# Decay sums of a gated linear attention by a VectorE scan in place of a triangular matmul, with two products re-ordered

## The chip, the cores and the metric

One Trainium2 chip, eight cores. The batch has eight sequences and every core computes one of them alone, with the whole set of weights; the cores exchange nothing. The metric is the device time in microseconds of the slowest core. Engines are named TensorE (PE), VectorE (DVE), ScalarE (ACT), GpSimd (POOL) and SyncE (SP). Each works off its own list of instructions.

## The reference

A layer of a decoder: a half-step SwiGLU, a mixer, cross-attention into 256 memory tokens, a second half-step SwiGLU, a final norm. Widths: model 1024, sequence 4096, hidden 2816. The change touches the mixer's gated linear attention alone. It has four heads with keys of 128 and values of 256, and computes, per head,

```
log_a = logsigmoid(a_code @ w_alpha + b_alpha) / 16          # per token and key channel
b     = cumsum(log_a) within a chunk                         # cumulative log decay
o     = (q*exp(b)) @ (k*exp(-b))^T (causal) @ v  +  (q*exp(b)) @ state
state = exp(b_last) * (state + (k*exp(-b))^T @ v)
o     = rmsnorm over the 256 values of a head, times silu(r)
```

The second line is what the change computes in another way. The kernel works in chunks of 128 tokens where the reference has 64; the value is the same.

## The kernel before, in words

**Tiling.** Activations lie transposed, channels on partitions and tokens along the free dimension. The sequence is cut into four tiles of T = 1024 tokens. Each tile goes through first SwiGLU, mixer, cross-attention and second SwiGLU. Weights stream from HBM into five slots of 1 MB (in bf16), by DMAs issued from GpSimd's queue.

**Order of the work.** There is no planner: `Sched` writes for every engine one list of instructions in the order in which the Python code calls `S.op` and `S.mm`, and puts a semaphore wait before an instruction where a buffer that it reads or writes was last touched by another engine. So the order of the calls is the order on each engine, and whoever stands behind a waiting instruction on its engine waits too.

**PSUM.** `psum()` (line 306) hands out the eight banks in turn. In the recurrence `first_bank[0] = 2`: banks 0 and 1 are kept for the chunk's output (`B_o`), and all other products share six banks in turn. A product must therefore wait until the product six places before it in the order of calls has been read out.

**The recurrence** (label mix/gla, the loop `for i in range(12)`) works on the eight chunks of a tile as a software pipeline. In step i it calls, in this order: `B_norm(i-4)` (sum of squares over a head on PE with `onesV`, Ln and Exp on ACT into `rsn`, and then two DVE products that scale the output from banks 0 and 1 into `ogT`); `A1(i)` (the forget-gate projection, one 512-column matmul, then Exp into `zb` and Ln into `lp` on ACT, which gives the negative log of the decay); a fill; `A2(i-1)` (four 128-column matmuls with the triangle `triB`, which sum `lp` over the tokens of the chunk; Exp into `eb` and into `enb` on ACT; on DVE q times `eb`, k times `enb`; on GpSimd a copy of the last column into `ebl`); a fill; `A3(i-2)` (four score matmuls and four transposes of k on PE, masking on DVE, copy into `kg` on ACT); `B_kv(i-3)` (four 256-column matmuls into two banks, four DVE updates of the state, a GpSimd product `Sbf`); in steps 3 to 8 another fill; `B_o(i-3)` (sixteen 128-column matmuls into banks 0 and 1, square on ACT into `osq`); from step 3 on another fill; in steps 0 to 3 `pool(3-i, 1)`, the trailing sums of the other branch, two to five DVE instructions.

**Fills** are whole projection groups for PE, eight 512-column matmuls and one read-out each, taken from a list: values of chunks 0 and 1, then q and k of the tile's second half in turn, values of chunks 2 to 7, then the output gate r. Read-outs of values and of r alternate between ACT and DVE (`evac`, line 582); those of q are on ACT, those of k on DVE. In steps 1 to 8 the first fill of a step is read out by ACT, the second by DVE, the third by ACT and the fourth by DVE.

Of the kernel before, what the change touches and what calls it, by code (L numbers as in the profile page):

```python
# [7 lines left out]
F32 = mybir.dt.float32  # L8
BF16 = mybir.dt.bfloat16
AF = mybir.ActivationFunctionType  # L10
ALU = mybir.AluOpType
# [156 lines left out]
def build_program(nt=SEQ // T):  # L168
    nc = bass.Bass("TRN2", target_bir_lowering=False)
    S = Sched(nc)  # L170
# [28 lines left out]
    def sb(name, shape, dt):  # L199
        return nc.alloc_sbuf_tensor("sb_" + name, list(shape), dt)  # L200
# [26 lines left out]
    wa = sb("wa", [128, 256], BF16)  # L227
    identB = sb("identB", [128, 128], BF16)
    triB = sb("triB", [128, 128], BF16)
    onesD = sb("onesD", [128, 128], BF16)  # L230
    onesV = sb("onesV", [128, 128], BF16)
    walpha = sb("walpha", [128, 512], BF16)
# [8 lines left out]
    def ov(name, off_k, shape, dt, nb=1):  # L241
        esz = 4 if dt == F32 else 2
        size = int(np.prod(shape[1:])) * esz
        lo = int(off_k * 1024)
        hi = lo + size
        assert hi <= ARENA, (name, hi)
        t = nc.alloc_sbuf_tensor_at("ov_" + name, list(shape), dt, offset=abase + lo)
        bufs = [Buf(f"{name}{i}") for i in range(nb)]
        for (l2, h2, b2) in overlay:
            if l2 < hi and lo < h2:  # L250
                for b in bufs:
                    for o in b2:
                        b.alias.append(o)
                        o.alias.append(b)
        overlay.append((lo, hi, bufs))
        return t, bufs
# [18 lines left out]
    ogT, og_b = ov("ogT", 49, [128, 8, T], BF16, nb=8)  # L275
    dfT, df_b = ov("dfT", 65, [128, 4, T], BF16, nb=8)
    aT, aT_b = ov("aT", 73, [128, T], BF16, nb=2)
    lp2 = [ov(f"lp{i}", 75 + i, [128, 512], BF16) for i in range(2)]
    zb2 = [ov(f"zb{i}", 77 + 2 * i, [128, 512], F32) for i in range(2)]
    eb2 = [ov(f"eb{i}", 81 + 2 * i, [128, 4, 128], F32) for i in range(2)]  # L280
    enb2 = [ov(f"enb{i}", 85 + 2 * i, [128, 4, 128], F32) for i in range(2)]
# [24 lines left out]
    def psum():  # L306
        lo = first_bank[0]
        i = lo + bank_rr[0] % (8 - lo)
        bank_rr[0] += 1
        return banks[i], bank_b[i]  # L310
# [27 lines left out]
    def xload(i, src, reads=()):  # L338
        st, b = xs[i]
        S.dma("pool", [(st[:], src)], reads, b, f"dma:xs{i}")  # L340
        return st, b[0]
# [14 lines left out]
    wa_b = Buf("walpha")  # L356
    cb2 = Buf("const2")
    S.op("dve", lambda e: e.memset(onesD[:], 1.0 / 1024.0), [], [cb2])
    S.op("dve", lambda e: e.memset(onesV[:], 1.0 / 256.0), [], [cb2])
    S.op("dve", lambda e: e.tensor_copy(out=identB[:], in_=small[:, O_IDENT:O_IDENT + 128]), [const_b], [cb2])  # L360
    S.op("dve", lambda e: e.tensor_copy(out=triB[:], in_=small[:, O_TRI:O_TRI + 128]), [const_b], [cb2])
    CB = [const_b, cb2]
# [306 lines left out]
    def mixer(t, n1):  # L669
# [11 lines left out]
        v4 = lambda ap: ap.rearrange("p (a b) -> p a b", a=4)  # L681
# [87 lines left out]

        def A1(c):  # L770
            zb, zb_b = zb2[c % 2]
            lp, lp_b = lp2[c % 2]
            bz, bzb = psum()
            S.mm([(bz[:], aT[:, c * 128:(c + 1) * 128], walpha[:], True, True)], [aT_b[c // 4], wa_b], [bzb])
            S.op("act", lambda e: e.activation(out=zb[:], in_=bz[:], func=AF.Exp, scale=-1.0), [bzb], zb_b)  # L775
            S.op("act", lambda e: e.activation(out=lp[:], in_=zb[:], func=AF.Ln, bias=1.0), zb_b, lp_b)

        def A2(c):
            lp, lp_b = lp2[c % 2]
            eb, eb_b = eb2[c % 2]  # L780
            enb, enb_b = enb2[c % 2]
            tk = slice(c * 128, (c + 1) * 128)
            bc, bcb = psum()
            S.mm([(bc[:, h * 128:(h + 1) * 128], lp[:, h * 128:(h + 1) * 128], triB[:], True, True) for h in range(4)],
                 lp_b + CB, [bcb])
            S.op("act", lambda e: e.activation(out=eb[:], in_=v4(bc[:]), func=AF.Exp, scale=-1.0 / 16.0), [bcb], eb_b)
            S.op("act", lambda e: e.activation(out=enb[:], in_=v4(bc[:]), func=AF.Exp, scale=1.0 / 16.0), [bcb], enb_b)
            S.op("dve", lambda e: e.tensor_tensor(out=qT[:, :, tk], in0=qT[:, :, tk], in1=eb[:], op=ALU.mult),
                 eb_b, [qT_b[c]])
            S.op("dve", lambda e: e.tensor_tensor(out=kTt[:, :, tk], in0=kTt[:, :, tk], in1=enb[:], op=ALU.mult),  # L790
                 enb_b, [kT_b[c]])
            S.op("pool", lambda e: e.tensor_copy(out=ebl[:, c, :], in_=eb[:, :, 127]), eb_b, [ebl_b[c]])

        def A3(c):
            tk = slice(c * 128, (c + 1) * 128)
            sm, sm_b = sm3[c % 3]
            kg, kg_b = kg3[c % 3]
            bs, bsb = psum()
            S.mm([(bs[:, h * 128:(h + 1) * 128], kTt[:, h, tk], qT[:, h, tk], True, True) for h in range(4)],
                 [kT_b[c], qT_b[c]], [bsb])  # L800
            bt, btb = psum()
            btv = bt[:].bitcast(BF16)
            S.tr([(btv[:, h * 128:(h + 1) * 128], kTt[:, h, tk], identB[:]) for h in range(4)], [kT_b[c]] + CB, [btb])
            S.op("dve", lambda e: e.tensor_tensor(
                out=v4(sm[:]), in0=v4(bs[:]), in1=triB[:].unsqueeze(1).to_broadcast([128, 4, 128]), op=ALU.mult),
                [bsb] + CB, sm_b)
            S.op("act", lambda e: e.activation(out=kg[:], in_=btv[:, 0:512], func=AF.Copy), [btb], kg_b)
# [38 lines left out]
        def B_norm(c):  # L846
            tk = slice(c * 128, (c + 1) * 128)
            bn, bnb = psum()
            oq = osq[:].rearrange("p (h v) i -> p h v i", v=2)
            S.mm([(v4(bn[:]), onesV[:], oq[:, :, vc, :], vc == 0, vc == 1) for vc in range(2)], osq_b + CB, [bnb])  # L850
            S.op("act", lambda e: e.activation(out=rsn[:], in_=v4(bn[:]), func=AF.Ln, bias=EPS), [bnb], rsn_b)
            S.op("act", lambda e: e.activation(out=rsn[:], in_=rsn[:], func=AF.Exp, scale=-0.5), [], rsn_b)
            og_ = ogT[:, :, tk].rearrange("p (h v) i -> p h v i", v=2)
            for vc in range(2):
                S.op("dve", lambda e, vc=vc: e.scalar_tensor_tensor(
                    out=og_[:, :, vc, :], in0=ovh[:, :, vc, :], scalar=small[:, O_GHEAD + vc:O_GHEAD + vc + 1],
                    in1=rsn[:], op0=ALU.mult, op1=ALU.mult), bank_b[0:2] + rsn_b + CB, [og_b[c]])
# [29 lines left out]
        def fill(n=1):  # L887
            lab = S.label
            S.label = "mix/fill"
            while todo and (n > 0 or todo[0][0] == "pre"):  # L890
                name, f = todo.pop(0)
                f()
                seen.add(name)
                if name != "pre":
                    n -= 1
            S.label = lab
# [2 lines left out]
        first_bank[0] = 2  # L899
        for i in range(12):  # L900
            heavy = 3 <= i <= 8
            if 0 <= i - 4 < 8:
                B_norm(i - 4)
            if i < 8:
                A1(i)
            fill()
            if 0 <= i - 1 < 8:
                A2(i - 1)
            fill()
            if 0 <= i - 2 < 8:  # L910
                A3(i - 2)
            if 0 <= i - 3 < 8:
                assert not any(n == f"v{i - 3}" for n, _ in todo)
                B_kv(i - 3)
            if heavy:
                fill()
            if 0 <= i - 3 < 8:
                B_o(i - 3)
            if i >= 3:
                fill()  # L920
            if i < 4:
                pool(3 - i, 1)
            if i == 9:
                pend["yb"] = xload(0, wpb_d, wpb_db)
                pend["gb1"] = xload(1, win_d[10])
# [178 lines left out]
    for t in range(nt):  # L1104
# [19 lines left out]
        hooks[(1, 6)].append(nx0.rest)  # L1124
        ffn(0, xin, hooks, nxt, mb if t == 0 else (), [mem_rest] if t == 0 else ())
        n1 = mixer(t, nx1)
        n1 = xattn(t, n1)
        S.label = "ffn1"
# [24 lines left out]
    for key in [f"dma:out{c}_{lo}" for c in range(2) for lo in range(0, 8, 2)]:  # L1153
        if key in S.dmacnt:
            b = Buf(key)
# [76 lines left out]
```

How the kernel before makes its waits and increments, by code:

```python
                def body(e, prog=prog, own=own):  # L154
                    for item in prog:
                        if item[0] == "wait":
                            e.wait_ge(self.semh[item[1]], item[2])
                        elif item[0] == "ins":
                            ins = item[1](e)
                            if item[2]:
                                ins.then_inc(own, 1)
                        else:
                            ins = item[1](e)
                            ins.then_inc(self.semh[item[2]], 16)
```

## Time and profile before

| | us |
|---|---|
| median of 3 runs | 3144.58 (3141.55 to 3508.37) |
| the profiled execution | 3143.91 |
| its span, slowest core (core 2) | 3142.0 |
| spans of the eight cores | 3133.7 to 3142.0 |
| PE busy | 3081.2 (98%) |
| DVE busy | 1185.6 (38%) |
| ACT busy | 950.6 (30%) |
| POOL busy | 480.5 (15%) |

Busy time is the time in which an instruction of the engine is in progress; matmuls overlap each other, so a single one shows 379 ns of which the next one hides the larger part. The interval between the starts of two rows is what an engine needs for the first of them when it has no wait. All rows below are of core 2.

### The profile page before, as it was taken

The numbers are of one execution on the slowest core, as the hardware profiler recorded it, in microseconds if no ns is written. First come the engines' busy times: TensorE is split into PE (matmuls) and PEld (weight loads), VectorE is DVE, ScalarE is ACT, GpSimd is POOL, SyncE is SP. The second block draws the span as 40 slices with busy tenths as digits, with TensorE's granted clock in tenths as the row PEclk, the third lists the DMA queues.
The fourth block names the chain that finished last, engine by engine and source line by source line (L and its number), as shares of the span: only waits on it lengthen the run. The fifth ranks groups of instructions, "written<-read, shape, count | busy, mean of one in ns | idle before, by whom it ended". The sixth has DMA issues, their size and how long they took to land.

```text
span 3142.0 us, 42848 instructions; the slowest of 8 cores (3133.7 to 3142.0 us)
## 1 busy us (share of the span) xinstructions
PE 3081.2 (98%) x15047; PEld 1448.3 (46%) x15350; DVE 1185.6 (38%) x1880; ACT 950.6 (30%) x1637; POOL 480.5 (15%) x557
## 2 busy tenths in 40 slices
PE   6999999999999999999999999999999999999998
PEld 2544544444444454444444445444444444544443
DVE  2223744522321473541332156363232226536212
ACT  3122532521211253342121136153212114425211
POOL 0012111121201120122110112022120021112002
PEclk9999999999999999999999999999999999999999
DMA  8797343344753634334384455233457344322434
GB/s 169 119 160 126 63 91 118 60 74 79 141 98 65 105 69 84 108 68 86 58 173 73 73 92 108 49 113 62 88 102 145 64 84 89 81 68 55 89 69 105
DMA packets 56784, 292.32 MB, mean 93 GB/s; under 512 B 5632, under 2 KB 11136, under 8 KB 32256
## 3 DMA queue, kind: packets, MB, share of 16 engines
q0 software_dynamic: 39024, 251.35, 44.4%
q1 hardware_dynamic: 17552, 38.21, 3.8%
q8 instruction: 129, 2.11, 0.3%
q14 instruction: 79, 0.65, 0.1%
HBM read 495.78 MB, written 22.02 MB: 165 GB/s over the span
## 4 chain that ended last, share of the span: by engine, by line
PE 95%; DMA 2%; issue 1%; DVE 1%; ACT 1%; DVEq 0%; SPq 0%; ACTq 0%; POOLq 0%
PE psum_all L107 95%; DMA sb_slot<-w_in 1%; DMA sb_slot<-ffn_w 1%; PE psum_all L123 1%; DMA ov_xin<-x 0%; DVE sb_hT L419 0%; DVE sb_xT L419 0%; ACT ov_rawb L388 0%; DVE ov_kT L790 0%; DVE ov_kT L702 0%; ACT ov_zb L775 0%; DVE ov_nmx L1021 0%; ACT ov_rstd L413 0%; ACT ov_rstd L411 0%; ACT ov_uT L692 0%
## 5 line engine op out<-in xcount | busy, mean ns | idle before, releaser
L107 PE MATMUL psum_all<-sb_hT,sb_slot 128*128 128x512 bf16 x7507 | 1678.9, 380 | 29.8 <-DMA sb_slot<-ffn_w 7.7
L107 PEld LDWEIGHTS psum_all<-sb_hT,sb_slot 128*128 128x128 bf16 x7680 | 750.3, 98 | 922.0 <-issue 35.1
L107 PE MATMUL psum_all<-ov_gated,sb_slot 128*128 128x512 bf16 x2760 | 608.7, 379 | 3.6 <-DMA sb_slot<-ffn_w 0.6
L520 DVE TENSOR_TENSOR ov_gated<-psum_all,ov_sl 128x512 bf16<-128x512 f32 x352 | 243.3, 691 | 922.1 <-PE psum_all L107 869.2
L517 ACT ACTIVATE ov_sl<-psum_all 128x512 bf16<-128x512 f32 x352 | 210.2, 597 | 906.1 <-PE psum_all L107 857.7
L107 PEld LDWEIGHTS psum_all<-ov_gated,sb_slot 128*128 128x128 bf16 x2816 | 275.5, 98 | 333.3 <-issue 1.6
L388 ACT ACTIVATE ov_sqt<-sb_xT 128x512 bf16<-128x512 f32 x224 | 140.4, 629 | 545.5 <-DVE sb_xT L541 215.4
L395 POOL TENSOR_TENSOR ov_acc<-ov_acc,ov_sqt 128x512 f32<-128x512 f32 x180 | 212.1, 1178 | 480.1 <-ACT ov_sqt L388 477.4
L135 POOL DMA_DIRECT2D sb_slot<-ffn_w x176 | 95.5, 544 | 1222.0 <-PE psum_all L107 1076.5
L107 PE MATMUL psum_all<-sb_slot,sb_hT 128*128 128x512 bf16 x1002 | 232.1, 379 | 1.6 <-ACT ov_uT L692 0.5
L419 DVE SCALAR_TENSOR_TENSOR sb_hT<-sb_xT,sb_small,ov_rstd 128x512 bf16<-128x512 f32 x192 | 140.8, 792 | 30.2 <-ACT ov_rstd L413 30.2
L946 ACT ACTIVATE ov_tg<-psum_all 128x512 f32<-128x512 f32 x128 | 74.6, 597 | 255.1 <-PE psum_all L107 247.6
L107 PEld LDWEIGHTS psum_all<-sb_slot,sb_hT 128*128 128x128 bf16 x1024 | 98.2, 98 | 106.4
L545 DVE SCALAR_TENSOR_TENSOR sb_xT<-psum_all,ov_xin 128x512 f32<-128x512 f32 x64 | 43.8, 690 | 225.8 <-PE psum_all L107 225.8
L960 DVE SCALAR_TENSOR_TENSOR ov_t<-ov_tg,psum_all 128x512 f32<-128x512 f32 x64 | 44.1, 688 | 207.5 <-PE psum_all L107 207.5
L107 PE MATMUL psum_all<-ov_ogT,sb_slot 128*128 128x512 bf16 x503 | 120.3, 379 | 0.5
L107 PE MATMUL psum_all<-ov_PT,sb_slot 128*128 128x512 bf16 x500 | 112.5, 379 | 0.6
L541 DVE SCALAR_TENSOR_TENSOR sb_xT<-psum_all,sb_xT 128x512 f32<-128x512 f32 x64 | 43.8, 689 | 180.9 <-PE psum_all L107 180.1
L107 PE MATMUL psum_all<-ov_mg,sb_slot 128*128 128x512 bf16 x500 | 111.2, 379 | 0.6
L822 POOL TENSOR_TENSOR Sbf<-S,sb_ebl 128x1024 bf16<-128x1024 f32 x32 | 60.5, 1892 | 135.3 <-DVE S L819 118.6
L107 PEld LDWEIGHTS psum_all<-ov_ogT,sb_slot 128*128 128x128 bf16 x512 | 50.1, 98 | 60.4
L107 PEld LDWEIGHTS psum_all<-ov_mg,sb_slot 128*128 128x128 bf16 x512 | 50.1, 98 | 59.7
(138 smaller groups left out, 1999.5 us busy)
## 6 DMA issues: line engine op xcount, KB each, us to landing
sb_slot<-ffn_w POOLq DMA_DIRECT2D x88, 1024.0 KB, 11.7
sb_slot<-ffn_w POOLq DMA_DIRECT2D x88, 704.0 KB, 7.3
sb_slot<-w_in POOLq DMA_DIRECT2D x40, 1024.0 KB, 13.1
out<-sb_xT SPq DMA_DIRECT2D x14, 1024.0 KB, 16.7
ov_xin<-x SPq DMA_DIRECT2D x12, 1024.0 KB, 13.7
sb_slot<-w_up_a POOLq DMA_DIRECT2D x8, 1024.0 KB, 13.1
sb_slot<-w_mix_out POOLq DMA_DIRECT2D x8, 1024.0 KB, 11.1
sb_slot<-kq_s POOLq DMA_DIRECT2D x8, 1024.0 KB, 5.1
```

The source lines that it names most:

```text
L107: ("ins", (lambda e, o=o, l=l, r=r, st=st, sp=sp: e.matmul(o, l, r, start=st, stop=sp)), i == n - 1)
L135: self.prog[queue].append(("dma", (lambda e, o=o, i=i: e.dma_start(out=o, in_=i)), key))
L388: S.op("act", lambda e: e.activation(out=t_[:, 0:w], in_=self.src[:, kc, :], func=AF.Square), sb_, tb)
L395: S.op("pool", lambda e: e.tensor_tensor(out=acc[:, 0:w], in0=acc[:, 0:w], in1=t_[:, 0:w], op=ALU.add), tb, self.acc_b)
L419: S.op("dve", lambda e, kc=kc: e.scalar_tensor_tensor(out=self.dst[:, kc, :], in0=self.src[:, kc, :], scalar=gvec(self.goff, kc), in1=rstd ...
L517: S.op("act", lambda e, b1=b1, slt=slt: e.activation(out=slt[:], in_=b1[:], func=AF.Silu), [bb1], [slb[0]])
L520: S.op("dve", lambda e, b3=b3, slt=slt, j=j, s=s: e.tensor_tensor(out=gated[:, j, sl(s)], in0=b3[:], in1=slt[:], op=ALU.mult), [bb3, slb[0 ...
L541: S.op("dve", lambda e, bk=bk, m=m, s=s: e.scalar_tensor_tensor(out=xT[:, m, sl(s)], in0=bk[:], scalar=0.5, in1=xT[:, m, sl(s)], op0=ALU.m ...
L545: S.op("dve", lambda e, bk=bk, m=m, s=s: e.scalar_tensor_tensor(out=xT[:, m, sl(s)], in0=bk[:], scalar=0.5, in1=x_in[s][0][:, m, :], op0=A ...
L822: S.op("pool", lambda e: e.tensor_tensor(out=Sbf2[c % 2][:], in0=S32[:], in1=ebl[:, c, :].unsqueeze(2).to_broadcast([128, 4, 256]), op=ALU ...
L946: S.op("act", lambda e, bk=bk, tg=tg: e.activation(out=tg[:], in_=bk[:], func=AF.Tanh, scale=0.5), [bb], tg_b)
L960: S.op("dve", lambda e: e.scalar_tensor_tensor(out=t1[:], in0=tga[:], scalar=1.0, in1=ba[:], op0=ALU.add, op1=ALU.mult), [bab] + tga_b, t1_b)
```

## The change

The triangular matmul and its PSUM bank go. `A1` makes the gate projection with the roles of its operands exchanged, four matmuls of 128 columns, one for each head, so that key channels come out on partitions and tokens along the free dimension; Ln now writes back into `zb` in float32. `A2` sums along the free dimension with one `tensor_tensor_scan` on DVE over 128x512 elements. For each element the scan multiplies the running value by a mask `segm` and adds `zb`; the mask is 1 but for a 0 at the first token of each head, so that the sum starts anew there. The result `cum` (float32 in SBUF) is what the two Exp on ACT read.

The order of calls changes too. `A2(i-1)` with the scan and the two Exp is now the first call of step i, ahead of `B_norm` and `A1`. The products with q and k and the copy into `ebl` become `A2b(i-1)`, at the place where `A2` stood. The two DVE products at the end of `B_norm` become `B_scale(i-4)`, after `A2b`.

```diff
+    segm = sb("segm", [128, 4, 128], BF16)
...
-    lp2 = [ov(f"lp{i}", 75 + i, [128, 512], BF16) for i in range(2)]
+    cum, cum_b = ov("cum", 75, [128, 512], F32)
...
+    S.op("dve", lambda e: e.memset(segm[:], 1.0), [], [cb2])
+    S.op("dve", lambda e: e.memset(segm[:, :, 0:1], 0.0), [], [cb2])
...
         def A1(c):
             zb, zb_b = zb2[c % 2]
-            lp, lp_b = lp2[c % 2]
             bz, bzb = psum()
-            S.mm([(bz[:], aT[:, c * 128:(c + 1) * 128], walpha[:], True, True)], [aT_b[c // 4], wa_b], [bzb])
+            S.mm([(bz[:, h * 128:(h + 1) * 128], walpha[:, h * 128:(h + 1) * 128], aT[:, c * 128:(c + 1) * 128], True, True)
+                  for h in range(4)], [aT_b[c // 4], wa_b], [bzb])
             S.op("act", lambda e: e.activation(out=zb[:], in_=bz[:], func=AF.Exp, scale=-1.0), [bzb], zb_b)
-            S.op("act", lambda e: e.activation(out=lp[:], in_=zb[:], func=AF.Ln, bias=1.0), zb_b, lp_b)
+            S.op("act", lambda e: e.activation(out=zb[:], in_=zb[:], func=AF.Ln, bias=1.0), [], zb_b)
 
         def A2(c):
...
-            bc, bcb = psum()
-            S.mm([(bc[:, h * 128:(h + 1) * 128], lp[:, h * 128:(h + 1) * 128], triB[:], True, True) for h in range(4)],
-                 lp_b + CB, [bcb])
-            S.op("act", lambda e: e.activation(out=eb[:], in_=v4(bc[:]), func=AF.Exp, scale=-1.0 / 16.0), [bcb], eb_b)
-            S.op("act", lambda e: e.activation(out=enb[:], in_=v4(bc[:]), func=AF.Exp, scale=1.0 / 16.0), [bcb], enb_b)
+            S.op("dve", lambda e: e.tensor_tensor_scan(
+                out=cum[:], data0=segm[:].rearrange("p a b -> p (a b)"), data1=zb[:], initial=0.0,
+                op0=ALU.mult, op1=ALU.add), zb_b + CB, cum_b)
+            S.op("act", lambda e: e.activation(out=eb[:], in_=v4(cum[:]), func=AF.Exp, scale=-1.0 / 16.0), cum_b, eb_b)
+            S.op("act", lambda e: e.activation(out=enb[:], in_=v4(cum[:]), func=AF.Exp, scale=1.0 / 16.0), cum_b, enb_b)
+
+        def A2b(c):
...
+        def B_scale(c):
+            tk = slice(c * 128, (c + 1) * 128)
             og_ = ogT[:, :, tk].rearrange("p (h v) i -> p h v i", v=2)
...
         for i in range(12):
             heavy = 3 <= i <= 8
+            if 0 <= i - 1 < 8:
+                A2(i - 1)
             if 0 <= i - 4 < 8:
                 B_norm(i - 4)
             if i < 8:
                 A1(i)
             fill()
             if 0 <= i - 1 < 8:
-                A2(i - 1)
+                A2b(i - 1)
+            if 0 <= i - 4 < 8:
+                B_scale(i - 4)
             fill()
```

## Rows read from the trace of the kernel before

**Rows 1.** The page's first part: busy us, share of the span, number of instructions

```profile
PE 3081.2 (98%) x15047; PEld 1448.3 (46%) x15350; DVE 1185.6 (38%) x1880; ACT 950.6 (30%) x1637; POOL 480.5 (15%) x557
```

**Rows 2.** The page's chain of work that ended last, by engine

```profile
PE 95%; DMA 2%; issue 1%; DVE 1%; ACT 1%; DVEq 0%; SPq 0%; ACTq 0%; POOLq 0%
```

**Rows 3.** Groups by line and shape: count, busy us, mean ns, idle before them

```profile
L788 DVE TENSOR_TENSOR ov_qT<-ov_qT,ov_eb 128x512 bf16<-128x512 bf16 x32 | 22.0, 686 | 6.9 <-ACT ov_eb L786 6.9
...
L1021 DVE TENSOR_REDUCE ov_nmx<-psum_all 128x4 f32<-128x1024 f32 x32 | 39.1, 1221 | 30.2 <-PE psum_all L107 30.2
...
L107 PE MATMUL psum_all<-sb_triB,ov_lp 128*128 128x128 bf16 x128 | 12.4, 219 | 0.0
```

**Rows 4.** Timeline of PE, step 7 of tile 0: start us, us, instruction

```profile
377.07 0.59 PE L107 MATMUL psum_all<-ov_osq,sb_onesV 128*128 128x512 bf16 x2
377.71 1.89 PE L107 MATMUL psum_all<-sb_slot,sb_hT 128*128 128x512 bf16 x8
379.44 0.39 PE L107 MATMUL psum_all<-sb_triB,ov_lp 128*128 128x128 bf16 x4
379.66 1.89 PE L107 MATMUL psum_all<-sb_slot,sb_hT 128*128 128x512 bf16 x8
381.39 0.39 PE L107 MATMUL psum_all<-ov_qT,ov_kT 128*128 128x128 bf16 x4
...
381.84 0.60 PE L107 MATMUL psum_all<-ov_vtok,ov_kg 128*128 128x256 bf16 x4
382.27 1.89 PE L107 MATMUL psum_all<-sb_hT,sb_slot 128*128 128x512 bf16 x8
...
386.62 0.59 PE L107 MATMUL psum_all<-ov_osq,sb_onesV 128*128 128x512 bf16 x2
```

**Rows 5.** Timeline of ACT in the same step

```profile
377.81 0.60 ACT L851 ACTIVATE ov_rsn<-psum_all 128x512 f32<-128x512 f32 x1 [1.19 <-PE psum_all L107]
378.50 0.63 ACT L852 ACTIVATE ov_rsn<-ov_rsn 128x512 f32<-128x512 f32 x1
379.04 0.58 ACT L775 ACTIVATE ov_zb<-psum_all 128x512 f32<-128x512 f32 x1
379.71 0.63 ACT L776 ACTIVATE ov_lp<-ov_zb 128x512 bf16<-128x512 f32 x1
380.25 0.58 ACT L585 ACTIVATE ov_vtok<-psum_all 128x512 bf16<-128x512 f32 x1
380.72 0.59 ACT L786 ACTIVATE ov_eb<-psum_all 128x512 f32<-128x512 f32 x1
```

**Rows 6.** Timeline of DVE in the same step

```profile
377.41 0.69 DVE L587 TENSOR_SCALAR ov_vtok<-psum_all 128x512 bf16<-128x512 f32 x1 [1.49 <-PE psum_all L107]
...
381.42 0.69 DVE L788 TENSOR_TENSOR ov_qT<-ov_qT,ov_eb 128x512 bf16<-128x512 bf16 x1 [0.58 <-ACT ov_eb L786]
```

**Rows 7.** Timeline of PE, tile 0: in step 3, and where step 4 begins

```profile
341.45 1.89 PE L107 MATMUL psum_all<-sb_hT,sb_slot 128*128 128x512 bf16 x8 [1.08 <-DVE ov_kT L702]
...
348.40 0.59 PE L107 MATMUL psum_all<-ov_osq,sb_onesV 128*128 128x512 bf16 x2
```

**Rows 8.** Timeline of DVE, steps 1 and 2 of tile 0

```profile
334.59 0.69 DVE L788 TENSOR_TENSOR ov_qT<-ov_qT,ov_eb 128x512 bf16<-128x512 bf16 x1
...
336.39 0.70 DVE L735 TENSOR_TENSOR ov_pwA<-ov_uT 128x527 f32<-128x527 f32 x1
...
339.42 0.68 DVE L788 TENSOR_TENSOR ov_qT<-ov_qT,ov_eb 128x512 bf16<-128x512 bf16 x1
...
340.62 0.68 DVE L702 CAST ov_kT<-psum_all 128x512 bf16<-128x512 f32 x1
```

**Rows 9.** Timeline of PE in the mixer of tile 1

```profile
1072.89 2.64 PE L107 MATMUL psum_all<-sb_hT,sb_slot 128*128 128x512 bf16 x8 [2.08 <-DMA sb_slot<-w_in]
```

**Rows 10.** Busy us by engine in a window just behind; last PEclk, DMA share, GB/s

```profile
1073.37:1076.79 3.42, 3.42 (x11) 1.27 (x10) 3.07 (x5) 0.00 (x0) 0.00 (x0) 0.57 1.05 163
```

More of the change, by code:

```diff
@@ L771, in A1 @@
             zb, zb_b = zb2[c % 2]
-            lp, lp_b = lp2[c % 2]
             bz, bzb = psum()
-            S.mm([(bz[:], aT[:, c * 128:(c + 1) * 128], walpha[:], True, True)], [aT_b[c // 4], wa_b], [bzb])
+            S.mm([(bz[:, h * 128:(h + 1) * 128], walpha[:, h * 128:(h + 1) * 128], aT[:, c * 128:(c + 1) * 128], True, True)
+                  for h in range(4)], [aT_b[c // 4], wa_b], [bzb])
             S.op("act", lambda e: e.activation(out=zb[:], in_=bz[:], func=AF.Exp, scale=-1.0), [bzb], zb_b)
-            S.op("act", lambda e: e.activation(out=lp[:], in_=zb[:], func=AF.Ln, bias=1.0), zb_b, lp_b)
+            S.op("act", lambda e: e.activation(out=zb[:], in_=zb[:], func=AF.Ln, bias=1.0), [], zb_b)
         def A2(c):
-            lp, lp_b = lp2[c % 2]
+            zb, zb_b = zb2[c % 2]
             eb, eb_b = eb2[c % 2]
@@ L782, in A2 @@
             tk = slice(c * 128, (c + 1) * 128)
-            bc, bcb = psum()
-            S.mm([(bc[:, h * 128:(h + 1) * 128], lp[:, h * 128:(h + 1) * 128], triB[:], True, True) for h in range(4)],
-                 lp_b + CB, [bcb])
-            S.op("act", lambda e: e.activation(out=eb[:], in_=v4(bc[:]), func=AF.Exp, scale=-1.0 / 16.0), [bcb], eb_b)
-            S.op("act", lambda e: e.activation(out=enb[:], in_=v4(bc[:]), func=AF.Exp, scale=1.0 / 16.0), [bcb], enb_b)
+            S.op("dve", lambda e: e.tensor_tensor_scan(
[4 more added lines that the diff above has]
+        def A2b(c):
+            eb, eb_b = eb2[c % 2]
+            enb, enb_b = enb2[c % 2]
+            tk = slice(c * 128, (c + 1) * 128)
             S.op("dve", lambda e: e.tensor_tensor(out=qT[:, :, tk], in0=qT[:, :, tk], in1=eb[:], op=ALU.mult),
@@ L852, in B_norm @@
             S.op("act", lambda e: e.activation(out=rsn[:], in_=rsn[:], func=AF.Exp, scale=-0.5), [], rsn_b)
+        def B_scale(c):
+            tk = slice(c * 128, (c + 1) * 128)
             og_ = ogT[:, :, tk].rearrange("p (h v) i -> p h v i", v=2)
```

## The prediction

> **What bounds the kernel now.** I read the busy shares first: PE is busy in 98% of the span, no other engine above 38% [rows 1], and the chain that ended last runs over PE for 95% [rows 2]. So a column taken from PE is worth its time in full, and every wait put before a PE instruction costs in full. Next the groups by line for the prices [rows 3], then the timelines of a step of the recurrence. A full step (here step 7) takes PE from 377.07 to 386.62, 9.55 us [rows 4], and there is no wait in it: two 512-column products and the gate projection take 0.64 us (377.07 to 377.71), each fill 1.73 (377.71 to 379.44), the triangle's four matmuls 0.22 (379.44 to 379.66), scores and transposes 0.45, `B_kv` 0.43. The only wait of PE that recurs in the recurrence is 1.08 us in step 3, for DVE's read-out of a k group (once in each tile, four in all) [rows 7]. DVE has no idle time before any row of steps 1 and 2 [rows 8], because the trailing sums of `pool` lie there.
>
> **The change, part by part.**
>
> *Taken from PE.* 128 matmuls of the triangle, 0.22 us for each group of four [rows 3, 4], 32 chunks: 7.0 us. *Gate projection:* four times 128 columns for one time 512. The columns are the same, and the triangle's four took 0.22 us for 512 columns as the long ones do (0.64 for three) [rows 4], so nothing. *Memsets:* two, once, at the start, under the first load of x: nothing; uncovered they would cost under 2 us.
>
> *The scan.* Not in the trace. One DVE pass of this size takes 0.69 us [rows 3]; that is the low end, since a sum over the tokens reads every element at least once. The high end is the 1.22 us of the reduction over twice as many elements [rows 3]. I take 1.22: the scan does a product and then a sum on the same running value and cannot overlap neighbours as the elementwise row does. DVE has room on average (in step 7 it is idle for 1.49 and 0.58 us [rows 6]); the question is who waits.
>
> *The order.* Before, the two decay exponentials stood behind the first fill's read-out on ACT and followed PE alone. Now they are the first two ACT instructions of a step and wait for DVE; behind them on ACT stand `B_norm`'s Ln and Exp, the new chunk's Exp and Ln, and the first fill's read-out. PE shares six banks in turn, nine or ten products in a step, so it needs these: the first `B_kv` product has the bank that `B_norm`'s Ln frees, the second that of the new chunk's Exp, the third fill that of the first fill. I follow this from row to row. Intervals on ACT: 0.69, 0.54, 0.67, 0.54 for Ln, Exp, Exp, Ln of a step [rows 5]; 0.53 for each decay exponential, which now reads SBUF as the row with 0.54 does; on DVE 0.60 per instruction [rows 8]. Handing over takes 0.11 from ACT to DVE (380.72 plus 0.59 to 381.42) [rows 5, 6], taken for the other way too, and 0.15 to PE (340.62 plus 0.68 to 341.45) [rows 7, 8].
>
> *Steps 5 to 7*, counted from the start of `B_norm`'s product. DVE reads out the last fill at 0.34 [rows 4, 6], starts the scan at 0.94, ends at 2.16. ACT: 2.27 and 2.80 the decay exponentials, 3.33 Ln, 4.02 Exp, 4.56 Exp of the gate (ends 5.14), 5.23 Ln, 5.77 first fill (ends 6.35). PE without the triangle would start `B_kv` at 4.55, its second product at 4.77, the third fill at 4.98. The second product waits until 5.29, the third fill until 6.50: stalls of 0.52 and 0.99. The step takes 9.55 - 0.22 + 1.51 = 10.84, +1.29; three steps +3.9. With a scan of 0.69, +0.77 each. *Step 8* has no gate projection: the first fill is out at 5.14, the third fill waits 0.52 from 4.77: +0.3 (cheap scan -0.2).
>
> *Steps 1 to 3.* The scan stands behind `pool` on DVE. Scan 0 starts where q times `eb` did, 334.59 [rows 8], the exponentials follow at 335.92, the score product waits until 338.0 and the transposes until 338.9 (1.4 of stall together). `pool` of step 1 takes 3.03 (336.39 to 339.42) [rows 8] and now ends at 341.5; scan 1 ends at 342.7, the gate's Exp of chunk 2 at 344.4, and q's next group, whose bank that Exp frees, starts at 344.55: a stall of 5.3. `pool` of step 2 ends at 348.1, scan 2 at 349.35; the second `B_kv` product waits 2.5 for the gate's Exp behind it, the third fill 1.1 more. Step 4, which began at 348.40 [rows 7], begins at 356.8: +8.4 with the old stall of 1.08 and three triangles taken off. With the cheap scan +6.8. *Step 4:* `pool` of step 3 and scan 3 delay ACT again: 0.9, 1.0 and 1.0 us before the two `B_kv` products and the third fill, +2.7 (cheap +2.2). From step 9 on there is neither a scan nor a decay exponential, and `B_scale` frees banks 0 and 1 two fills ahead of `B_o`: nothing.
>
> Per tile 8.4 + 2.7 + 3.9 + 0.3 = 15.3, four tiles 61 us (cheap scan 11.0 and 44). The 7 us from PE are in this sum.
>
> *The clock.* In tile 1 PE stood for 2.08 us and behind that the granted clock was at its lower level, 1.2 GHz (0.57 over a window whose edges belong to the upper level) for 3.4 us [rows 9, 10]: some 1.7 us lost; none of the four stalls of 1.08 shows that. Behind the 5.3 us stall a loss is hidden, since the next stall waits for DVE and ACT anyway. The stalls of 2.5 and 1.1 follow each other closely and nothing behind them absorbs a loss; nor is it absorbed in step 4. I take one loss of 1.7 per tile, 7 us; none and two are the bounds, 0 and 14.
>
> *Sum:* 3143.9 + 61 + 7 = 3212 for the profiled execution; the median stands 0.7 above that execution, which changes nothing.
>
> On the scan's price the Trainium skill has a rule, in DVE: opcode table, instruction layouts, handler registers and perf-mode slots, section Datapath and trigger behaviour: handing a running value back to an earlier stage costs bubbles, and the built-in scan runs at half throughput. By it the scan is an estimated 1.22 us (the row of 0.69 with 512 elements' time added once more, at the reduction's pace), the dear end, and the sum is 3212 instead of 3188 to 3195. It speaks against the change; no row of the trace before shows a scan.
>
> **The rivals.**
>
> *The scan is cheap (0.69).* The same stalls, shorter: +44, with up to 7 for the clock: 3188 to 3195. For it: every DVE row of 512 elements has this price, whatever it computes. Chance 0.2.
>
> *The ends come together differently, and the change gains.* If the scan is done before PE needs what stands behind it on ACT, only the 7 us remain: 3137. It decides in steps 5 to 7 at one point: the scan must end 1.5 us earlier, at 0.65, when the last fill's read-out has hardly begun; and in steps 1 to 3 `pool` must not stand before it. For it: ACT and DVE are busy for about a third of the span [rows 1]. Against it: the order of calls leaves no such place. This is the case on the other side. Chance 0.07. That the stalls come but only as large as the gain (some buffer is freed sooner than I see), 3145 to 3175: 0.07.
>
> *The clock falls in every step with stalls, or the scan is dearer than 1.22.* A loss of 1.7 in steps 5 to 7 too would add 5 per tile, 20 in all, to the 14: 61 + 34 = 95, 3239. A scan of 2.4 us adds about 1.2 to each of eight steps: 38, 3250. For it: stalls of 1.5 us in each step, against 2.08 where the clock did fall. Against it: four stalls of 1.08 without a fall. Chance 0.14.
>
> *The forecast,* with 0 to 14 for the clock, 3205 to 3219: 0.52.
>
> **The numbers.** Predicted 3212. The range 3180 to 3245 leaves out the gain, the small stalls and the dearest scan. Within 2% means 3082 to 3207, about what a measurement of this kernel can tell from no change. Faster by more is excluded by PE's own columns but for a mistake: 0.01. Within it lie the cheap scan (0.2), the gain and small stalls (0.14) and the lower edge of the forecast, where the clock costs nothing or a stall is shorter than worked out (0.14): 0.48. Slower 0.51.
>
> **What would show it.** The scan's mean duration, 1.22 or 0.69. PE's waits: one of about 5 us in each tile ended by ACT's gate Exp, 20 us in all; waits for `zb` and for the first fill's read-out in steps 3 to 7; the wait for DVE's k read-out gone. ACT's idle time before the first decay exponential ended by `cum`, and PE's step of 9.55 grown to about 10.8. In steps 9 to 11 nothing changes. The granted clock at its lower level once or twice per tile. I would be wrong if PE's six banks do not bind it to ACT in this way, which would show as steps of 9.33 without waits.

## The result and the profile after

The changed kernel is slower by 2.2%: ratio 1.0225 with an interval of 1.0208 to 1.0242. The profiled execution took 3214.66 us where 3212 was forecast, 70.8 us above the profiled execution of before. (The medians over all executions, 3316.75 against 3326.47, are swollen on both sides by executions in which a die ran at a lower clock; the ratio leaves these out.) The rows of after are of its slowest core, core 7; those of every run below are of the slowest core of that run.

The page's first part and the chain that ended last, after; they answer to [rows 1, 2].

```profile
PE 3110.5 (97%) x15318; PEld 1443.4 (45%) x15318; DVE 1223.1 (38%) x1914; ACT 947.4 (29%) x1637; POOL 487.7 (15%) x557
...
PE 91%; DVE 3%; ACT 2%; issue 2%; DMA 2%; SPq 0%; DVEq 0%; POOL 0%; ACTq 0%; POOLq 0%
```

The busy shares hardly show anything: DVE has 37.5 us more, and PE's share fell by one point. The chain shows it: PE has 91% of it instead of 95%, and DVE and ACT, 1% each before, have 5% together. Next the groups for the scan and for the new gate projection, against [rows 3].

```profile
L786 DVE TENSOR_TENSOR_SCAN ov_cum<-sb_segm,ov_zb 128x512 f32<-128x512 bf16 x32 | 38.9, 1216 | 0.0
...
L107 PE MATMUL psum_all<-ov_aT,sb_walpha 128*128 128x128 bf16 x128 | 12.5, 221 | 1.7 <-DVE ov_vtok L590 1.7
```

The scan takes 1.22 us, the dear end. The four matmuls of the projection are as cheap as the triangle's four were (221 against 219 ns each).

PE's waits after the change (waiting engine and tile, what it waited for, us in total, times, the longest). Only waits of the recurrence are shown. Before, one wait of the recurrence stood there, four times for DVE's k read-out, 4.3 us in all [rows 7].

```profile
PE psum_all L107 <- ACT ov_zb L778: 32.1, 24, 5.9
...
PE psum_all L107 <- ACT ov_vtok L588: 9.9, 12, 0.8
...
PE psum_all L107 <- ACT ov_qT L700: 6.6, 8, 0.8
PE psum_all L107 <- DVE ov_kT L798: 3.6, 4, 0.9
PE psum_all L107 <- ACT ov_rsn L859: 3.1, 4, 0.8
PE psum_all L107 <- DVE ov_vtok L590: 1.7, 4, 0.4
PE psum_all L107 <- DVE ov_ogT L866: 1.6, 4, 0.4
```

Everything that stands on ACT behind the two decay exponentials is there: the gate's Exp (`zb`), the head norm's Ln (`rsn`), the first fill's read-out (`vtok`, `qT`). The wait for the k group's read-out (line 705 now) is gone. One of the waits for `zb` in each tile is the long one of step 3, 5.4 to 5.9 us.

Step 5 of tile 0 on PE, against step 7 of [rows 4]:

```profile
373.05 0.59 PE L107 MATMUL psum_all<-ov_osq,sb_onesV 128*128 128x512 bf16 x2
373.48 0.39 PE L107 MATMUL psum_all<-ov_aT,sb_walpha 128*128 128x128 bf16 x4
373.70 3.62 PE L107 MATMUL psum_all<-sb_slot,sb_hT 128*128 128x512 bf16 x16
377.15 0.39 PE L107 MATMUL psum_all<-ov_qT,ov_kT 128*128 128x128 bf16 x4
...
377.60 0.38 PE L107 MATMUL psum_all<-ov_vtok,ov_kg 128*128 128x256 bf16 x2
378.34 0.38 PE L107 MATMUL psum_all<-ov_vtok,ov_kg 128*128 128x256 bf16 x2 [0.36 <-ACT ov_zb L778]
379.55 1.89 PE L107 MATMUL psum_all<-sb_slot,sb_hT 128*128 128x512 bf16 x8 [0.83 <-ACT ov_vtok L588]
...
383.89 0.38 PE L107 MATMUL psum_all<-ov_osq,sb_onesV 128*128 128x512 bf16 x1
```

The step takes 10.84 us (373.05 to 383.89, where the view ends after the first of two matmuls), not 9.55. A bracket shows less than what is lost, since the matmul before it is still draining: from start to start the second `B_kv` product is late by 0.52 (378.34 less 377.60 less 0.22) and the third fill by 0.99 (379.55 less 378.34 less 0.22).

The same step on DVE and ACT, against [rows 5, 6]:

```profile
373.39 0.69 DVE L590 TENSOR_SCALAR ov_vtok<-psum_all 128x512 bf16<-128x512 f32 x1 [1.78 <-PE psum_all L107]
374.00 1.21 DVE L786 TENSOR_TENSOR_SCAN ov_cum<-sb_segm,ov_zb 128x512 f32<-128x512 bf16 x1
```

```profile
375.36 0.63 ACT L789 ACTIVATE ov_eb<-ov_cum 128x512 f32<-128x512 f32 x1 [2.76 <-DVE ov_cum L786]
...
376.41 0.58 ACT L859 ACTIVATE ov_rsn<-psum_all 128x512 f32<-128x512 f32 x1
...
377.62 0.58 ACT L778 ACTIVATE ov_zb<-psum_all 128x512 f32<-128x512 f32 x1
...
378.82 0.58 ACT L588 ACTIVATE ov_vtok<-psum_all 128x512 bf16<-128x512 f32 x1
```

ACT was idle for 2.76 us. Behind the exponential that waited stood the head norm's Ln and the gate's Exp, whose inputs PE had delivered before 374, and then the read-out; PE now waits for the last two of these, one after another.

### The profile page after: what moved, and what is told of

Read it like the earlier page. It is cut to its first block, busy times and chain, and to the rows that moved or that the text cites. A ratio compares the mean times of both kernels' runs of the same rounds, so it can differ in the third digit from the quotient of the medians.

```text
span 3212.7 us, 43076 instructions; the slowest of 8 cores (3202.5 to 3212.7 us)
## 1 busy us (share of the span) xinstructions
PE 3110.5 (97%) x15318; PEld 1443.4 (45%) x15318; DVE 1223.1 (38%) x1914; ACT 947.4 (29%) x1637; POOL 487.7 (15%) x557
## 4 chain that ended last, share of the span: by engine, by line
PE 91%; DVE 3%; ACT 2%; issue 2%; DMA 2%; SPq 0%; DVEq 0%; POOL 0%; ACTq 0%; POOLq 0%
PE psum_all L107 90%; DMA sb_slot<-w_in 1%; DVE ov_cum L786 1%; PE psum_all L123 1%; DMA ov_xin<-x 0%; ACT ov_enb L790 0%; DVE ov_vtok L590 0%; DVE ov_pwA L738 0%; ACT ov_zb L778 0%; DVE ov_pwB L738 0%; ACT ov_vtok L588 0%; ACT ov_rsn L859 0%; DVE ov_ogT L866 0%; DVE ov_dfT L741 0%; DVE sb_xT L422 0%
## 5 line engine op out<-in xcount | busy, mean ns | idle before, releaser
L107 PE MATMUL psum_all<-sb_hT,sb_slot 128*128 128x512 bf16 x7680 | 1697.9, 381 | 40.6 <-ACT ov_zb L778 22.2
```

Source lines behind the costliest of these rows:

```text
L107: ("ins", (lambda e, o=o, l=l, r=r, st=st, sp=sp: e.matmul(o, l, r, start=st, stop=sp)), i == n - 1)
```

## The experiments

The theory: the loss is a wait. PE waits for ACT (through the six shared banks), ACT for the scan at the head of its queue, and the scan for what stands before it on DVE. Rivals: the scan's own time on DVE is the loss, wherever it stands; the moved q, k and output products are; the clock is.

**1. The scan in the old order.**

```diff
-            if 0 <= i - 1 < 8:
-                A2(i - 1)
             if 0 <= i - 4 < 8:
                 B_norm(i - 4)
+                B_scale(i - 4)
...
             if 0 <= i - 1 < 8:
+                A2(i - 1)
                 A2b(i - 1)
-            if 0 <= i - 4 < 8:
-                B_scale(i - 4)
```

> The scan stays, but the calls stand in the order of before: A2 with A2b behind the first fill, B_scale directly behind B_norm. If the loss comes from what waits behind the scan on ScalarE (the new chunk's Exp and the first fill's read-out), it goes in steps 4 to 8, where a step takes about 9.5 us again, and the wait of 5.5 us for the gate's Exp is gone; what stays is VectorE's backlog of trailing sums plus scans in steps 1 to 3, some 5 to 6 us per tile, with 0 to 2 per tile for the clock: 3165 to 3180. If the 38.9 us of scan on VectorE are the cost wherever they stand, the time stays at 3207 to 3214.

3172.48 us in the profiled execution, 28.6 above that of before. Steps 5 to 7 take 9.50 us. What stays is in steps 1 to 3, 5.6 to 6.0 us per tile, and in step 4, 1.7 to 1.9, which I had expected to be free; PE, tile 0:

```profile
338.11 0.38 PE L107 MATMUL psum_all<-ov_qT,ov_kT 128*128 128x128 bf16 x4 [0.84 <-DVE ov_kT L798]
...
345.49 0.59 PE L107 MATMUL psum_all<-ov_qT,ov_kT 128*128 128x128 bf16 x4 [3.04 <-DVE ov_kT L705]
...
363.67 1.89 PE L107 MATMUL psum_all<-sb_slot,sb_hT 128*128 128x512 bf16 x8 [1.96 <-DVE ov_kT L705]
```

So 42 of the 71 us come from the place of the calls, with every scan still there. The rest is DVE's backlog: PE now waits for k's product with `enb` and for k's read-out, behind the trailing sums and the scans. Behind the wait of 3.04 the granted clock was at its lower level too (0.50 over 346 to 351), so a part of the rest can be the clock; no run separates it. The rival that the scan's 38.9 us cost wherever they stand falls.

**2. The order without the scan.** The triangle's matmuls and `lp` are back, inside `A2` at the front:

```diff
         def A2(c):
-            S.op("dve", lambda e: e.tensor_tensor_scan(
-                out=cum[:], ...
+            bc, bcb = psum()
+            S.mm([(bc[:, h * 128:(h + 1) * 128], lp[:, h * 128:(h + 1) * 128], triB[:], True, True) for h in range(4)],
+                 lp_b + CB, [bcb])
```

> The order of the changed kernel without the scan: the triangle's matmuls and lp are back, A2 with them stands at the front of the step, A2b and B_scale stand where the change put them. If the scan at the front is the cause, the two decay exponentials now wait for four short matmuls only, steps 5 to 7 take 9.55 us, and only B_scale's later place costs (0.57 us in step 10, 2.3 in all): 3145 to 3149. If moving the exponentials, the q and k products or B_scale is what costs, the time is at 3170 or above.

Ratio 1.0007 (0.9996 to 1.0019), profiled execution 3146.37. Steps 5 to 7 take 9.55 us. The order alone costs nothing but one small wait, in step 10, which has no second fill between `B_scale` and `B_o` that could hide it (only one fill stands between them from step 9 on):

```profile
411.04 0.22 PE L107 MATMUL psum_all<-ov_sm,ov_vtok 128*128 128x128 bf16 x1 [0.41 <-DVE ov_ogT L866]
```

Step 10 takes 7.51 us in place of 6.94. The rival that the moved products cost falls. Neither the place (this run) nor the scan in steps 5 to 8 (run 1) costs much alone; the place costs 2.5 us without the scan and 42 with it.

**3. The scan one step early.** It is taken out of `A2` and called in step i for chunk i, behind `A3`:

```diff
+        def A2s(c):
+            zb, zb_b = zb2[c % 2]
+            S.op("dve", lambda e: e.tensor_tensor_scan(...), zb_b + CB, cum_b)
...
             if 0 <= i - 2 < 8:
                 A3(i - 2)
+            if i < 8:
+                A2s(i)
```

> The scan of chunk i is called in step i behind A3, ahead of the trailing sums, and the rest of A2 stays at the front of step i+1, so that the exponentials find the sum ready. If waiting is the cause, steps 5 to 7 take 9.33 us and the first PE wait for the gate's Exp is gone; VectorE is still overfull in steps 1 to 3 and holds PE by about 3 us per tile there: 3148 to 3160. If the scan's own time is the cost, 3200 or above.

Ratio 1.0052 (1.0034 to 1.0070), profiled execution 3159.86. PE, step 5 of tile 0, has no wait left and takes 9.33 us (364.50 to 373.83), the 9.55 less the triangle's 0.22:

```profile
364.50 0.59 PE L107 MATMUL psum_all<-ov_osq,sb_onesV 128*128 128x512 bf16 x2
...
365.15 3.62 PE L107 MATMUL psum_all<-sb_slot,sb_hT 128*128 128x512 bf16 x16
...
373.83 0.59 PE L107 MATMUL psum_all<-ov_osq,sb_onesV 128*128 128x512 bf16 x2
```

In steps 4 to 7 the scan runs every step and costs nothing. What is left is again the overfull DVE in steps 1 to 3, where PE still waits for the gate's Exp (14.1 us in eight waits, the longest 2.5): those three take 4.4 us more than before in tiles 1 to 3 (6.0 in tile 0), where I expected 3. The granted clock fell once in these steps of each tile (0.50 over 350 to 353 in tile 0); how much of the 4.4 that is, no run shows.

**4. A cheaper instruction in the scan's place.**

```diff
-            S.op("dve", lambda e: e.tensor_tensor_scan(
-                out=cum[:], data0=..., data1=zb[:], initial=0.0, op0=ALU.mult, op1=ALU.add), zb_b + CB, cum_b)
+            S.op("dve", lambda e: e.tensor_tensor(
+                out=cum[:], in0=segm[:].rearrange("p a b -> p (a b)"), in1=zb[:], op=ALU.mult),
+                zb_b + CB, cum_b)
```

> In place of the scan an elementwise product of the same operands (the sum is left out, so the decays are those of single tokens), 0.69 us where the scan has 1.22; nothing else differs from the changed kernel. By the working of the prediction the stall per step goes by the scan's end: steps 5 to 7 take about 10.3 us in place of 10.84, step 8 loses its stall, in all 16 to 20 us less: 3190 to 3200. If the place alone costs whatever the duration (a fixed handing over between engines), the time stays at 3210 to 3214.

The kernel leaves out the sum; nothing else differs from the changed one. Ratio 1.0174 (1.0158 to 1.0190), profiled execution 3196.36. The gate's Exp is in time for `B_kv`, so the stall of 0.52 is gone; the third fill still is 0.99 late. The step takes 10.32 us (369.16 to 379.48):

```profile
369.16 0.59 PE L107 MATMUL psum_all<-ov_osq,sb_onesV 128*128 128x512 bf16 x2
...
373.71 0.60 PE L107 MATMUL psum_all<-ov_vtok,ov_kg 128*128 128x256 bf16 x4
375.13 1.89 PE L107 MATMUL psum_all<-sb_slot,sb_hT 128*128 128x512 bf16 x8 [0.82 <-ACT ov_vtok L588]
...
379.48 0.59 PE L107 MATMUL psum_all<-ov_osq,sb_onesV 128*128 128x512 bf16 x2
```

A DVE instruction shorter by 0.53 us (0.683 for 1.216) makes the step shorter by 0.52: it lies on the path in full. It also shows that a scan at the price of an elementwise instruction would not have saved the change.

**5. Two scans in a row.** `A2` issues the scan twice, with the same result.

> The changed kernel with every scan issued twice, one behind the other, with the same result. By the working of the prediction each of the eight steps with a scan is later by the scan's 1.14 us from start to start, steps 5 to 7 take 11.98 us, and the four tiles lose 36 us more, up to 20 more where the clock falls: 3250 to 3270. If part of the wait is hidden anyway, less than half of that: 3232 or below.

3281.0 us in the only execution of this kernel, above the range that I gave. In step 5 of tile 1 the clock stayed at its upper level, and the step took 12.18 us (1179.49 to 1191.67), 1.34 more than with one scan where I expected 1.14 (the second scan, 1.225 us, also has to wait for the first to write). In step 5 of tile 0 it took more than that: the third fill and the output's matmuls, from 385.22 to 389.44, took 4.22 us where 1187.32 to 1189.94 took 2.62.

```profile
384.01 0.38 PE L107 MATMUL psum_all<-ov_vtok,ov_kg 128*128 128x256 bf16 x2 [0.83 <-ACT ov_zb L778]
385.22 2.72 PE L107 MATMUL psum_all<-sb_slot,sb_hT 128*128 128x512 bf16 x8 [0.83 <-ACT ov_vtok L588]
389.44 1.73 PE L107 MATMUL psum_all<-sb_slot,sb_hT 128*128 128x512 bf16 x7
...
1186.12 0.38 PE L107 MATMUL psum_all<-ov_vtok,ov_kg 128*128 128x256 bf16 x2 [0.83 <-ACT ov_zb L778]
1187.32 1.89 PE L107 MATMUL psum_all<-sb_slot,sb_hT 128*128 128x512 bf16 x8 [0.83 <-ACT ov_vtok L588]
1189.94 1.89 PE L107 MATMUL psum_all<-sb_slot,sb_hT 128*128 128x512 bf16 x8
```

The windows over the two stretches show the cause by the column behind POOL's, the granted clock: 0.88 and 1.00.

```profile
376.90:390.70 13.80, 11.44 (x67) 6.19 (x66) 8.70 (x13) 5.92 (x10) 2.61 (x2) 0.88 0.34 72
1178.90:1191.10 12.20, 9.84 (x68) 5.18 (x67) 8.70 (x13) 5.85 (x10) 1.41 (x2) 1.00 0.34 71
```

The three stalls (12.18 less 9.34, 2.84 us in a step) are the same in both, and yet the clock fell in one and not in the other: of the twelve steps 5 to 7 of this kernel ten took 13.84 to 14.14 us, and two, in tile 1, took 12.18. In the changed kernel, with 1.5 us of stalls in such a step, it fell in none of the twelve. So the rival of the prediction, that the clock falls in every step with stalls, did not hold for the change, but nearly does with stalls twice as long.

**6. The last wait of the kernel before.** Not a part of the change, but of the same queue: k groups of the fills are read out by ACT.

```diff
         def k_group(m, s):
             bk, bb = group(wk_, m, s)
-            S.op("dve", lambda e: e.tensor_copy(out=kTt[:, m, sl(s)], in_=bk[:]), [bb], kT_b[s * 4:s * 4 + 4])
+            if s == 1:
+                S.op("act", lambda e: e.activation(out=kTt[:, m, sl(s)], in_=bk[:], func=AF.Copy), [bb], kT_b[s * 4:s * 4 + 4])
+            else:
+                S.op("dve", lambda e: e.tensor_copy(out=kTt[:, m, sl(s)], in_=bk[:]), [bb], kT_b[s * 4:s * 4 + 4])
```

> The kernel before with one edit: in the recurrence's fills the k groups are read out by ScalarE in place of VectorE. The wait of 1.08 us for that read-out in step 3 of each tile goes; if nothing else is late there, 4.3 us less, 3139 to 3141. If VectorE's backlog only shows up at the next product (the mask or the q and k products), no change, 3143 to 3145.

Profiled execution 3137.07, below the range. No wait for the k read-out is left in the trace and the recurrence of a tile is shorter by 1.24 us, 5.0 of the 6.8 in four tiles; the other 1.8 lie outside it and aren't the edit's by any run. The comparison of whole runs, 0.9996 (0.9979 to 1.0014), can't tell it from nothing; the trace can.

**7. The scan only where DVE has room.** The kernel before in its own order; chunks 3 to 7 use the scan, called one step early, and chunks 0 to 2 the triangle.

```diff
+        NTRI = 3
...
-            bc, bcb = psum()
-            S.mm([(bc[:, h * 128:(h + 1) * 128], lp[:, h * 128:(h + 1) * 128], triB[:], True, True) for h in range(4)],
-                 lp_b + CB, [bcb])
+            if c >= NTRI:
+                bc, bcb = cum, cum_b[0]
+            else:
+                bc, bcb = psum()
+                S.mm([(bc[:, h * 128:(h + 1) * 128], lp[:, h * 128:(h + 1) * 128], triB[:], True, True) for h in range(4)],
+                     lp_b + CB, [bcb])
...
                 A3(i - 2)
+            if NTRI <= i < 8:
+                A2s(i)
```

> The kernel before, its order of calls kept, with the scan only for chunks 3 to 7 of a tile and called one step early, behind A3; chunks 0 to 2, whose steps have the trailing sums on VectorE, keep the triangle. If VectorE's backlog in steps 1 to 3 is all that spoils the early scan, steps 4 to 8 take 9.33 us and nothing is lost: 5 triangles of 0.22 us less in each of four tiles, 4.4 us less, 3138 to 3141. If a scan beside the state updates delays PE as well, 3144 or above.

Profiled execution 3139.30; whole runs 1.0008 (0.9966 to 1.0049), which again can't tell. Steps 6 to 8 are shorter by 0.21 to 0.23 us each, step 5 by 0.10, and step 4 is 0.10 longer (0.30 in tile 0): a read-out of k on DVE is late once more in each tile, behind the scan. The recurrence of a tile is shorter by 0.5 to 0.7 us where I expected 1.1, so only some 2.5 of the 4.6 us by which the profiled execution is shorter are the edit's.

**8. Both.**

> The two edits together (scan from chunk 3 on, k read out by ScalarE). If they are independent, 4.3 and 4.4 us add up: 3134 to 3137. If ScalarE, which now has the k read-outs too, becomes late for the gate's Exp, one of the two is lost: 3139 or above.

Ratio 0.9963 (0.9934 to 0.9992), faster than the kernel before and than the changed one; profiled execution 3134.32, 9.6 us under that of before, and single executions down to 3132.31. With k's read-outs gone from DVE the late read-out of run 7 is gone too: steps 4 to 7 all take 9.34 us. The recurrence of a tile is shorter by 2.2 to 2.4 us, slightly more than the 1.24 and 0.5 to 0.7 of the two edits apart, and PE waited for ACT nowhere in it. PE's waits in the whole kernel, from the longest to the shortest; none is left in the recurrence:

```profile
PE psum_all L107 <- DVE sb_hT L423: 13.5, 4, 7.1
PE psum_all L107 <- ACT ov_rawa L392: 9.8, 3, 7.3
PE psum_all L107 <- DMA sb_slot<-ffn_w: 1.9, 3, 1.4
PE psum_all L107 <- DMA sb_slot<-w_in: 1.6, 1, 1.6
PE psum_all L107 <- ACT ov_sqt L392: 1.6, 1, 1.6
```

## Where the prediction held and where it failed, point by point

The mechanism, the path and the scan's price were right, and for the profiled execution the number was too, but partly by luck. Three terms failed: the wait of `B_o` in step 10 (put at nothing), a wait of DVE in step 1 (not seen), and the clock, whose 7 us made up for these two. And the prediction put the median 0.7 above the profiled execution, "which changes nothing": that step failed too, since the four executions took 3213.61, 3214.66, 3418.84 and 3482.80 us and their median, 3316.75, is outside the range of 3180 to 3245.

*PE's gain* of 0.22 us per chunk is real. Run 3 shows it bare, 9.33 for 9.55. The gate projection costs the same as four matmuls, as assumed.

*The scan's price*, taken at the dear end for want of a row, was 1.216 us. The Trainium skill (DVE: opcode table, instruction layouts, handler registers and perf-mode slots, section Datapath and trigger behaviour) says that the built-in scan runs at half throughput. The estimate by that rule was 1.22: the trace agrees.

*Steps 5 to 7*: forecast 10.84 with stalls of 0.52 and 0.99; measured 10.84, 0.52 and 0.99 (11.13 in one step of twelve, step 7 of tile 1). *Step 8*: +0.3 forecast, 9.58 for 9.34 measured. *Step 4*: +2.7 forecast, 12.27 for 9.56 in tile 0. Its three stalls can be seen in the waits at 0.8 us each (brackets; about 1.0 from start to start).

*Steps 1 to 3*: +8.4 without the clock. Measured in tile 0 from the first gate projection to `B_norm` of step 4 (31.7 us against 22.3), +9.4 with the clock; 9.5, 10.1 and 9.9 in the other tiles. The large wait:

```profile
342.61 0.38 PE L107 MATMUL psum_all<-ov_aT,sb_walpha 128*128 128x128 bf16 x4 [0.41 <-DVE ov_vtok L590]
348.50 5.80 PE L107 MATMUL psum_all<-sb_hT,sb_slot 128*128 128x512 bf16 x16 [5.50 <-ACT ov_zb L778]
```

5.7 us from start to start beyond the 0.2 of the projection, for 5.3 forecast (5.2 by the forecast's own times). The next one, 2.5 by the forecast, shows as 0.27 only: PE was slow at the time (two fills took 5.6 us in place of 3.5) and arrived later.

*The first miss.* The large wait ended 1.0 us later than worked out (348.50, where 344.55 moved by the 2.94 us between the two traces is 347.49), and the reason is on DVE, in its work for step 1:

```profile
340.17 0.69 DVE L798 TENSOR_TENSOR ov_kT<-ov_kT,ov_enb 128x512 bf16<-128x512 bf16 x1
341.78 0.69 DVE L590 TENSOR_SCALAR ov_vtok<-psum_all 128x512 bf16<-128x512 f32 x1 [0.92 <-ACT ov_vtok L588]
...
345.41 1.22 DVE L786 TENSOR_TENSOR_SCAN ov_cum<-sb_segm,ov_zb 128x512 f32<-128x512 bf16 x1
```

```profile
341.09 0.58 ACT L588 ACTIVATE ov_vtok<-psum_all 128x512 bf16<-128x512 f32 x1
```

The forecast let `pool` of step 1 follow k's product and the value read-out without a gap, and end at 341.5. But the two read-outs of a chunk's values go into one buffer of the program (`v_b[blk]`), so that DVE's waits for ACT's, although they write different halves; and ACT's now stands behind the scan's exponentials. DVE waits 0.92, 0.92, 1.20 and 0.92 us in the four tiles, 4.0 in all, and in tile 0 it has no gap from there to the end of the scan, so `pool`, the scan and PE's wait all end later by that. No run takes this wait out alone; that it is on the path is read from the rows.

*The clock.* The granted clock fell at the start of the large wait or during it, in every tile, and was still at its lower level behind it; in tile 0:

```profile
345.70:352.40 6.70, 3.90 (x10) 1.46 (x11) 5.67 (x9) 3.23 (x6) 0.71 (x1) 0.53 0.00 0
```

As forecast this was hidden: the 2.2 us that PE lost in the two fills came out of the next wait. A second fall, behind the three stalls of step 4, occurred on this core in tile 1 alone:

```profile
1149.26 0.38 PE L107 MATMUL psum_all<-ov_vtok,ov_kg 128*128 128x256 bf16 x2 [0.79 <-ACT ov_rsn L859]
1150.46 0.38 PE L107 MATMUL psum_all<-ov_vtok,ov_kg 128*128 128x256 bf16 x2 [0.83 <-ACT ov_zb L778]
1151.67 3.56 PE L107 MATMUL psum_all<-sb_slot,sb_hT 128*128 128x512 bf16 x8 [0.83 <-ACT ov_qT L700]
1155.96 1.89 PE L107 MATMUL psum_all<-sb_slot,sb_hT 128*128 128x512 bf16 x8
```

The fill at 1151.67 shows 3.56 us where the next shows 1.89; that step took 13.93 us, 1.66 more than in tile 0.

*The second miss.* I wrote that `B_scale` frees its banks two fills ahead of `B_o` and costs nothing. From step 9 on there is one fill between them, and in step 10 it does cost. There the first fill is read out by DVE, `B_scale` stands behind that read-out, and `B_o` waits: 7.51 for 6.94 us, 0.57 per tile, 2.3 in all. Run 2 has the same 7.51 without a scan. The step failed because I looked at one parity of the alternating read-outs and not at the last steps'.

*The sum.* From the first gate projection to the last `B_norm` the four tiles take 16.8, 18.8, 17.4 and 17.2 us more than the 84.2 of before: 70.3, of 70.8 in all. Of it 61 are the stalls forecast less the gain, 2.3 the wait in step 10, 4.0 DVE's wait in step 1, and 1.7 the clock's second fall in tile 1. About 1 us is left, most of it in steps 1 to 3 of tiles 2 and 3; its cause is open. So the clock, put at 7, shows 1.7, and the two waits that the forecast lacked are 6.3. Two errors of 5 and 6 us cancelled: that the sum came to within 3 us of the profiled execution is luck to that extent.

*The rivals.* The cheap scan was tried as run 4: 3196.36, 1.4 above the 3188 to 3195 worked out, and its step 10 has the missed wait too. (The reason given for this rival, that every DVE row of 512 elements costs 0.69, isn't so: the `SCALAR_TENSOR_TENSOR` of line 419 with 128x512 elements took 0.79 before.) The gain needed the scan ready in time at the front of ACT's queue: run 3 makes that happen in steps 4 to 7, and these are the 9.33 us of that rival; the whole stays above before, since steps 1 to 3 do not come right.

## What to carry to other kernels

Ask of a moved instruction not only what it costs but who stands behind it. With the same scan a step took 10.84 us where it stood at the head of a queue that PE needs for its banks, and 9.33 where it was called half a step earlier. Work taken from the bounding engine is paid out only if the engine that takes it over is not late in that very stretch; DVE was at 38% over the span before and had no gap from 330.15 to 348.08 in tile 0, which is nearly all of steps 1 to 3. And where read-outs alternate between two engines, follow both parities to the last step; where they fill one buffer in turn, one waits for the other.

## What the runs showed of the hardware

A `tensor_tensor_scan` of 128x512 with a float32 input and a bfloat16 mask takes 1.216 us, beside 0.683 for an elementwise product of the same operands (run 4). Four matmuls of 128 columns take the same 0.22 us as one of 512, with four weight loads in place of one. ACT reads 512 float32 elements from SBUF in 0.63 us and from PSUM in 0.59. The clock fell to 1.2 GHz also behind stalls that came in three pieces of 0.7 to 0.8 us each (by their brackets) with matmuls between them (tile 1 above and run 5), not only behind one long wait; but it did not fall behind the same three pieces in two steps of run 5, nor in step 4 of the changed kernel's other tiles. Where it fell, the step grew by 1.66 us (13.84 against 12.18 in run 5, 13.93 against 12.27 in the changed kernel).
